# First up stage of a two-block transformer kernel: the high weights multiply the high and low rows in one 512-column product, and VectorE adds the halves of the bank ahead of the root

## What is computed

```python
h = rmsnorm(x, norm_ffn_pre[l])
u = causal_depthwise_conv(h @ w_ffn_up[l], ffn_conv_w[l], ffn_conv_b[l])
u_gate, u_val = jnp.split(u, 2, axis=-1)
y = (jax.nn.gelu(u_gate, approximate=True) * u_val) @ w_ffn_down[l]
x = x + rmsnorm(y, norm_ffn_post[l])
```

## Time and profile before

| | |
|---|---|
| median of 3 runs | 2490.61 us (2489.26 to 2491.90) |
| profiled execution | 2492.55 us, its span 2490.8 us |
| mean granted TensorE clock | 0.995 |
| TensorE busy | 2463.4 us (99%), 13692 matmuls |
| VectorE busy | 1397.8 us (56%) |
| ScalarE busy | 1092.9 us (44%) |
| GpSimd busy | 1348.1 us (54%) |
| memory read | 361.49 MB, 146 GB/s over the span |

### The profile page before, as it was taken

How to read it: one execution, slowest core, us unless ns; L and a number is a source line. 1 busy time by engine, 2 the same in 40 slices (tenths; PEclk the granted TensorE clock), 3 DMA queues, 4 the chain that set the end, 5 groups by cost and what they waited for, 6 DMA issues and landing times.

```text
span 2490.8 us, 40326 instructions
## 1 busy us (share of the span) xinstructions
PE 2463.4 (99%) x13692; PEld 2131.5 (86%) x13692; DVE 1397.8 (56%) x3218; ACT 1092.9 (44%) x2052; POOL 1348.1 (54%) x693
## 2 busy tenths in 40 slices
PE   9999999999999999999999999999999999999999
PEld 8889899988888888788888888888888888899888
DVE  5576666378884513555666555665554364655331
ACT  5474565543323433577262222342222343685554
POOL 5638788844444443454434444444444454666886
PEclk9999999999999999999999999999999999999999
DMA  7728456555654432122334444544443453335564
GB/s 245 242 90 261 154 173 189 179 161 191 202 159 133 141 102 77 60 73 65 118 102 152 144 138 131 165 131 152 152 146 100 142 172 126 102 103 169 169 203 135
DMA packets 407171, 364.12 MB, mean 146 GB/s; under 512 B 7564, under 2 KB 398302, under 8 KB 407056
## 3 DMA queue, kind: packets, MB, share of 16 engines
q1 hardware_dynamic: 384840, 339.21, 43.3%
q10 hardware_dynamic: 22216, 23.39, 2.9%
HBM read 361.49 MB, written 1.08 MB: 146 GB/s over the span
## 4 chain that ended last, share of the span: by engine, by line
PE 89%; POOL 4%; issue 3%; DVE 2%; DMA 1%; ACT 1%; POOLq 0%; SPq 0%; DVEq 0%; ACTq 0%
PE bank L2353 69%; PE bank L2363 5%; POOL w_lo L891 4%; PE bank L2361 3%; PE bank L3047 2%; PE bank L3089 1%; PE bank L2461 1%; PE bank L2468 1%; PE bank L2462 1%; PE bank L3075 1%; PE bank L2609 1%; PE bank L2360 1%; PE bank L2614 1%; PE bank L2610 0%; PE bank L2988 0%
## 5 line engine op out<-in xcount | busy, mean ns | idle before, releaser
L891 POOL TENSOR_TENSOR w_lo<-raw,w_hi 128x1024 fp32r<-128x1024 f32 (+3 forms) x557 | 1212.1, 2188 | 1008.7 <-ACT w_hi L970 1007.8
L2353 PE MATMUL bank<-u_both,w_hi 128*128 128x512 f32 (+1 forms) x4240 | 1091.1, 347 | 4.1 <-POOL w_lo L891 3.2
L970 ACT ACTIVATE w_hi<-raw 128x1024 fp32r<-128x1024 f32 (+3 forms) x558 | 533.6, 974 | 1010.6 <-PE bank L2353 797.5
L2353 PEld LDWEIGHTS bank<-u_both,w_hi 128*128 128x128 f32 x4240 | 739.1, 190 | 107.5 <-issue 6.4
L2353 PE MATMUL bank<-u_both,w_lo 128*128 128x512 f32 (+1 forms) x2120 | 733.1, 346 | 0.0
L2353 PEld LDWEIGHTS bank<-u_both,w_lo 128*128 128x128 f32 x2120 | 402.1, 190 | 48.9
L1792 DVE SCALAR_TENSOR_TENSOR bank<-mod_raw,cond,bank 128x256 f32<-128x256 f32 x1008 | 401.2, 481 | 0.3 <-DMA mod_raw<-in_w_mod 0.3
L2353 PE MATMUL bank<-hid_hi,w_hi 128*128 128x512 f32 x528 | 205.7, 390 | 0.0
L2353 PE MATMUL bank<-hid_hi,w_lo 128*128 128x512 f32 x528 | 205.4, 389 | 0.0
L2353 PE MATMUL bank<-hid_lo,w_hi 128*128 128x512 f32 x528 | 205.4, 389 | 0.0
L2133 DVE TENSOR_TENSOR bank<-bank,work 128x512 f32<-128x512 f32 (+1 forms) x88 | 55.5, 630 | 193.9 <-PE bank L2353 186.9
(11 more groups left out here) (333 smaller groups left out, 3663.0 us busy)
## 6 DMA issues: line engine op xcount, KB each, us to landing
mod_raw<-in_w_mod SPq DMA_DIRECT2D x144, 512.0 KB, 4.6
raw<-in_ffn_w_in SPq DMA_DIRECT2D x69, 1024.0 KB, 5.1
raw<-in_w_in SPq DMA_DIRECT2D x67, 1024.0 KB, 5.2
raw<-in_ffn_w_out SPq DMA_DIRECT2D x56, 704.0 KB, 4.5
raw<-in_w_ffn_up SPq DMA_DIRECT2D x22, 1024.0 KB, 5.0
raw<-in_ffn_w_in ACTq DMA_DIRECT2D x19, 1024.0 KB, 5.5
raw<-in_w_attn_out SPq DMA_DIRECT2D x8, 1024.0 KB, 5.0
raw<-in_w_o SPq DMA_DIRECT2D x8, 1024.0 KB, 4.9
```

Source lines behind the costliest of these rows:

```text
L891: pool.tensor_tensor(st.half(t, w_lo[slot]), st.half(t, block), st.half(t, w_hi[slot]).bitcast(f32), ALU.subtract).then_inc(lo_ready, 1)
L970: act.activation(st.half(t, w_hi[(st.first + c) % 2]), st.half(t, raw_of(st, n)), ACT.Copy).then_inc(hi_ready, 1)
L2353: ins = pe.matmul(dst, s, v, start=first and n == 0, stop=final and n == 2)
```

## The change

For the ten loop bodies of up1 TensorE uses `apart_three` (the argument `both=`). For each tile ScalarE copies the bank's upper half to `work` (`copy_half`, L1015), behind the high half of the weights for that tile, and in the last body's second block ahead of them; VectorE waits for the copy, adds it to the lower half in place, waits for its own add, and then multiplies by the root as before. The plan counts 40 such tiles, and the first body's VectorE work is taken out of the loop.

```diff
-    gemm("up1", pairs(a["w_ffn_up"][0]), 22)
+    gemm("up1", pairs(a["w_ffn_up"][0]), 22, apart=40)
@@ ScalarE
-            gemm("up1", conv_tiles, table=ACT.Gelu_apprx_tanh, first=first_conv)
+            gemm("up1", conv_tiles, table=ACT.Gelu_apprx_tanh, first=first_conv, apart=True)
@@ VectorE, scale_rows
                 dve.wait_ge(group_done, st.done(i, b + 1))
                 product = bank[b][:, 0:S]
+                if not isinstance(i, int):
+                    n = i * 4 + (st.apart0 + b - 3)
+                    dve.wait_ge(apart_copied, n)
+                    dve.tensor_tensor(product, product, work[:, b, S:T], ALU.add).then_inc(apart_summed, 1)
+                    dve.wait_ge(apart_summed, n)
                 dve.tensor_tensor(product, product, row_root, ALU.mult).then_inc(conv_scaled, 1)
@@ VectorE
-            gemm("up1", conv_ffn)
+            gemm("up1", conv_ffn, first=lambda st: conv_ffn(st, 0))
@@ TensorE
-            gemm("up1", features(*u_of(x_cols), S), late=rows_unnormed)
+            gemm("up1", features(*u_of(x_cols), S, both=both_of(x_cols)), late=rows_unnormed)
```

## The result

The kernel after takes 2504.40 us (median of 6 runs, 2502.43 to 2506.13), the kernel before 2489.94 in the same sessions (2488.02 to 2493.47). The ratio is 1.0056, with a 95% interval of [1.0046, 1.0066]: 14.5 us, 0.56% slower, where the forecast was a shift of 17.8 us. Ratios and their intervals are taken over all runs of both kernels, so that a ratio isn't exactly that of the two medians. The profiled execution of after took 2502.43 us, its span is 2500.6 at a mean granted clock of 0.998.

A forecast was written before the change was run, and what follows sets the result against it. Bound: TensorE at 11.54 us a body and an equal VectorE-ScalarE cycle of 11.53. The cycle growing to 13.02 and the tail give 16.2 us, the clock 1.6: 17.8 on 2490.61 makes 2508.4 us, range 2502 to 2514.

The forecast's parts named there:

- TensorE gains 0.36 a body, if left alone: In up1's loop the new products would need 11.18 us a body instead of 11.54, 3.6 us less in all.
- The closed cycle of 11.53: In up1's bodies VectorE and ScalarE take turns in an 11.53 us cycle beside TensorE's 11.54, so VectorE's idle time isn't free.
- First half +0.56, add to its multiply 0.56: From X (body's first root multiply; with the change, its first add) to D (fourth conv pass's end): 4.10 us for 3.54.
- Second half +0.93: From D (end of a body's fourth conv pass) to the next X (next body's start on VectorE): 8.92 us for 7.99.
- A body of 13.02: Each up1 loop body grows by 1.49 us to 13.02, with TensorE waiting for banks 0 and 2.
- The tail, +2.06: In up1's last body the split of down1's block 1 comes 2.06 us later behind D, 16.2 with the loop's 14.16.
- The clock, 1.6 us: After a 3.9 us TensorE wait at down1's block 1, a lowered clock costs 1.6 us.
- The covered adds: Rival: VectorE's 38 idle us in up1 are usable, TensorE sets 11.18 us a body, 3.6 us less, 2487.0; chance 5%.
- The free self-wait: Rival: VectorE's add to its multiply takes 0.34 us, not 0.56; a body 12.58, time 2503.7 us; chance 8%.
- A clock that takes over the loop: Rival: waits in up1's bodies lower TensorE's clock, a body takes 14.5 us, 15 us more, 2523; chance 5%.
- The signs of being wrong: In up1: copies later than the split order says, ScalarE waiting for a late refill before a copy, or TensorE without waits.

The follow-up runs named there:

- the products alone: Kernel before with only the 512-column products, no copies or adds, so low rows' share missing: 2490.13 us against 2489.34, ratio 1.0001.
- products and Gelus moved: Kernel before with the 512-column products (no copies or adds) and both Gelus behind the taps of banks 2 and 3: 2485.55 us, ratio 0.9987.
- the pair of experiments: On the kernel before, Gelus moved behind the taps of banks 2 and 3: ratio 0.9999; the same plus the 512-column products without copies or adds: 0.9987.
- the run with the copies first: Changed kernel with both copies ahead of both high halves in each loop body's second block: 2501.00 us, ratio 1.0050.

## Why the prediction was right, and where its sizes were off

The forecast was 2508.4 us with a range of 2502 to 2514; measured are 2504.4. That is inside the range, but below the 2506.5 to 2512 that the prediction gave its own mechanism: the shift is 14.5 us where 17.8 were forecast. The prediction had the mechanism and the sign right, and most of its sizes too large. Point by point:

- **TensorE gains 0.36 a body, if left alone.** Not seen in after, as it waits. With the products alone TensorE's weight loads wait for 4.1 us in ten bodies, and with products and Gelus moved the body falls from 11.54 to 11.21: confirmed.
- **The closed cycle of 11.53.** Confirmed by the pair of experiments in which each edit alone brings nothing and both together 3.3 us. It was the step that decided the sign, and no busy share shows it.
- **First half +0.56, add to its multiply 0.56.** Measured 0.46 to 0.49, and 0.46 to 0.47 for the step. This is the term that was mis-sized, for four adds in each body. I took it from the last up stage, where the multiply has a second wait as well; the trace of after shows how such gaps differ (last section).
- **Second half +0.93.** Measured 0.94, in part by luck. The shorter add-multiply steps should have brought the pass of bank 2 forward; the rows have multiply 3 at D + 3.47 and the pass at D + 3.81, against 3.47 and 3.87. What was gained at the steps was lost at the second copy: its add starts 0.47 behind it and not 0.39, at D + 3.00 for 2.91. The 0.06 gained at the pass is lost behind it: from there to the next X are 5.12 us instead of the 5.05 of before.
- **A body of 13.02.** 12.94: over nine bodies 0.7 us less. The waits for the conv passes came where they were forecast, at two banks, and with 1.84 us a steady body for 1.8; they are those of the weight loads, the products themselves wait once, for 1.15.
- **The tail, +2.06.** Measured 1.66. Half of the difference is the shorter step from add to multiply (0.19), half the tap, which in the last body starts 0.47 behind its multiply and not 0.69 (0.22). For the same two reasons the last body's X to D is 3.79 for 4.10. With 0.57 less ahead of the first X, which I had taken as unchanged though the change takes that body's VectorE work out of the loop, 0.16 less at the hand-over and the shorter bodies, 16.2 come down to 14.07. The wait at block 1 is 2.46 instead of 3.9 us.
- **The clock, 1.6 us.** It didn't come. This is the table by stretches of after behind the wait:

```profile
444.00:448.00 4.00, 3.74 (x22) 3.31 (x23) 3.57 (x9) 2.67 (x5) 4.00 (x4) 1.00 0.17 42
```

- The granted clock is 1.00, 2.4 GHz, where the stretch behind the 2.34 us wait of before has 0.58. So the length of the wait, by which I reasoned, doesn't decide alone. The very wait of the earlier trace rows shows it too: all twelve profiled executions have it, 2.23 to 2.61 us long and ahead of the same products. In the four us behind it the granted clock is 0.57 to 0.69 in six of them and 1.00 in the other six, after among these, with the longest of the waits (until 92.99). This is the stretch of the earlier trace rows in after:

```profile
95.00:99.00 4.00, 4.00 (x38) 4.00 (x37) 0.00 (x0) 1.51 (x4) 2.63 (x2) 1.00 1.01 308
```

- Behind the hand-over's own wait it is 1.00 both here and in the run with the copies first, where that wait is 2.50 us. The term should have stood in the sum as a chance, by these executions of about one half or less, and not as a full 1.6 us. What decides from execution to execution stays open.
- **Rivals.** The covered adds (2487) fell: the idle time of VectorE was no room. The free self-wait (12.58 a body) fell as well, but the truth lies between it and my value: 0.46, with 0.34 and 0.56 as the ends. The time alone wouldn't have told them apart: its 2503.7 is nearer to the measured 2504.4 than my 2508.4, and without the clock's 1.6 us it would be 2502.1 and mine 2506.8. The Trainium skill, VectorE: DVE Perf Modes, section "The DRAIN you can't avoid", has the semaphore costing nothing extra. This trace doesn't agree: the wait for the step before costs 0.12 a time. A clock that takes over the loop fell: 1.00 in all bodies, in spite of a wait of about 1.15 us in eight of them.
- **The signs of being wrong.** One of them came literally: ScalarE waits 1.87 us for a refill ahead of the first loop body's first copy (316.32). Before has the same wait, 1.88 us at 318.78, and the first X starts without a wait in both, so it cost nothing.

Copies and adds each cost less than their own busy time would say (four copies and four adds), because most of it does fall into idle time. What counts is what stands between X and D and between D and the next X: 0.47 for one add and its multiply in the first half, 0.63 for the copies in the second, and 0.30 for their order.

What stays open: what decides the clock behind a wait, and why the first loads and the clock of the first 20 us differ between two executions of the same work.

## What to carry to other kernels

Before new work is put into an engine's idle time, follow one loop body around all engines: if two of them hand work to and fro in a period as long as the bound's, the idle time between the hand-overs is latency, and every step added on that path lengthens the loop. Two bounds of equal length hide each other, so an edit that is worth nothing alone (here one moved pair of Gelus) may be worth 15 us beside another; test them together, and take other steps out of the cycle before giving up the edit that lengthened it. And don't take an engine's long waits for the bound: ScalarE waited 36.5 us for loads beside ten bodies in which TensorE didn't wait at all.

## What the runs showed of the hardware that I had not expected

The gap between two VectorE steps of which the second waits for the first isn't one number. In after the first body's VectorE work is written out ahead of the loop; in before the same work is the loop's first round, where addresses and waited values come from registers. A cast and the subtraction behind it, first in after, then in before:

```profile
316.23 0.42 DVE L2064 CAST hid_both<-bank 128x256 fp32r<-128x256 f32 x1
316.68 0.42 DVE L2066 TENSOR_TENSOR hid_both<-bank,hid_both 128x256 fp32r<-128x256 f32 x1
...
319.12 0.42 DVE L2064 CAST hid_both<-bank 128x256 f32 x1
319.69 0.43 DVE L2066 TENSOR_TENSOR hid_both<-bank,hid_both 128x256 f32 x1
```

The same lines on the same features, the same busy time, but 0.45 apart with constants and 0.57 with registers; in the loop bodies of after they are 0.57 apart too (432.23 and 432.80). The add and multiply of the change wait for the register value n that the line above has computed already, and are 0.46 apart. That the 0.56 of the earlier trace rows comes from a register computation ahead of the multiply fits these rows, but is only argued.

TensorE kept the 2.4 GHz through a wait of 2.46 us, through one of 2.61 and through eight of about 1.15, and fell to a mean of 0.58 behind one of 2.34. The same wait in the same place was followed by the low clock in six profiled executions and by the full one in six, so a single trace doesn't price it.
